# Two chained norms of a residual from sums over the chunks; add, scaling and split chunk by chunk; four chunks of the next map side by side

## The chip, the cores and the metric

The kernel runs on one core of a Trainium2 chip. The metric is the device time of a whole launch in microseconds. Most of the work is on TensorE (matmul); VectorE (DVE in the views) and ScalarE (ACT) prepare its operands and empty its PSUM tiles, SyncE issues the weight loads and GpSimd a few others.

## The reference, cut to what matters

Two diffusion-transformer layers are followed by a third, different block. The residual stream x has 512 latent tokens of 1024 features and, in layer 0, 256 context tokens beside them (768 columns in layer 0, 512 in layer 1). Each layer has two residual additions, and each is followed at once by the norm in front of the next linear map:

```python
xl_new = xl + ml[2] * rmsnorm(y_l, g_post_mix[i])
h2 = modulate(rmsnorm(xl_new, g_pre_mlp[i]), ml[3], ml[4])
xl_new = xl_new + ml[5] * rmsnorm(sqrelu_mlp(h2, w_mlp_in[i], w_mlp_out[i]), g_post_mlp[i])
...
hl = modulate(rmsnorm(xl, g_pre_mix[i]), ml[0], ml[1])   # next layer
zl = hl @ w_in[i]
```

`rmsnorm(u, g)` is `u * rsqrt(mean(u*u) + 1e-6) * g`, the mean over the 1024 features, and `modulate(h, shift, scale)` is `h * (1 + scale) + shift`. All is fp32.

## The kernel before, in words

**Layout.** Features lie on partitions: x is the SBUF tile `X` of 8 chunks of 128 features, each with up to 768 token columns; a branch's output is `Y` of the same form. A sum over features is thus a sum over the 8 chunks and, inside one, over partitions, which a matmul with a tile of ones does.

**Linear maps.** Both operands of a map are split in a high and a low part (`HH`, `HL` for activations, `AHm`, `ALm` inside the MLP, `WH`, `WL` for weights), and three matmuls (lines 555 to 557) stand for one fp32 product. Weights come in slabs of 128x2048; for each slab ScalarE writes `WH` (line 437) and VectorE `WL` (line 448). There are two buffers of each, so a slab can be split only when the last output chunk of the slab two before it is done. A map (`Linear`) makes its output chunks one after the other; with `pair` the first two are made side by side, input chunk by input chunk, so that the map can begin before all eight input chunks are ready. The PSUM ring `psum` has four tiles, one for each chunk under way.

**A residual.** `y` is evicted, squared on ScalarE, the squares are summed over chunks on VectorE (line 616), one matmul with ones sums over partitions (line 624), ScalarE makes `Ln` and then `Exp(-0.5 ...)` of it (lines 651, 658; each with a table load). `vector_add_normed` adds the normed y to X (lines 722, 715); ScalarE squares the new X (line 602), TensorE sums chunk by chunk (line 635), again `Ln` and `Exp`, and `vector_norm_split` scales (line 695) and makes `HL` (line 686), ScalarE `HH` (line 671). Only then the next map starts.

**Order.** Every engine runs an order written out by hand (the functions `tensor_*`, `scalar_*`, `vector_*`), and waits on semaphores; a wait holds all that stands behind it on the engine. The modulation products ("mods", line 477) of the next layer are woven into the weight plan, one behind each slab.

**Names of the stretches.** A is the residual after the mixer of layer 0 (next map: the first `up` map of the MLP), B that after the MLP of layer 0 (next: `w_in` of layer 1), C and D the same two of layer 1 (next: first `up` map, then `win2` of the third block). The MLP is done in 8 groups g; each has an `up` map (4 chunks, 2 slabs) and a `down` map (8 chunks, 2 slabs) that adds to Y. Between them the `up` chunks go through `Relu` on ScalarE (line 1339, which frees the PSUM tile), a square on VectorE (1391), `AHm` on ScalarE (1343) and `ALm` on VectorE (1395), with two buffers `TA`.

Of the kernel before, what the change touches and what calls it, by code (L numbers as in the profile page):

```python
# [529 lines left out]

def tensor_linear(k, pe, L, ring=None):
    ring = ring or k.psum
    for s, g in L.groups():
        if s is not None:
            n = k.slab_of[L.name, s]
            wh, wl = split_views(k, n, L.K)
            mods = list(k.mods[L.name, s])  # L540
# [26 lines left out]
def scalar_linear(k, act, L):  # L567
    for s, g in L.groups():
        if s is not None:
            n = k.slab_of[L.name, s]  # L570
            mods = list(k.mods[L.name, s])
            scalar_split(k, act, n)
            scalar_split(k, act, n + 1)
# [8 lines left out]
def vector_linear(k, dve, L):  # L582
    for s, g in L.groups():
        if s is not None:
            n = k.slab_of[L.name, s]
            mods = list(k.mods[L.name, s])
            vector_split(k, dve, n)
            vector_split(k, dve, n + 1)
# [118 lines left out]
def vector_add_normed(k, dve, name, segs, scale):  # L707

    a, b = span(segs)
    r = k.RS.of(name)  # L710

    def add(c):
        dve.wait_ge("norm_t", (name, c, segs[-1][0]))
        t = k.TD.of((name, c))
        dve.e.tensor_tensor(k.X[:, c, a:b], k.X[:, c, a:b], t[:, a:b], ALU.add).then_inc(*dve.done("x_new", (name, c)))

    for c in range(8):
        t = k.TD.take(dve, (name, c), ("x_new", (name, c)))
        dve.wait_ge("rstd", name)
# [66 lines left out]
def tensor_start(k, pe):  # L786
# [4 lines left out]
    for c in range(8):  # L791
        tensor_stat(k, pe, ("x", 0), c, 8, [LAT, CTX])
# [2223 lines left out]
```

## Time and profile before

| | us |
|---|---|
| median of 3 runs | 4177.93 (4172.32 to 4181.32) |
| the profiled execution, its time | 4172.92 |
| the profiled execution, its span | 4171.6 |
| TensorE busy | 3933.1 (94%) |
| VectorE busy | 2139.4 (51%) |
| ScalarE busy | 1514.4 (36%) |

The span runs from the first to the last instruction; 1.3 us of the launch lie outside it. TensorE is busy almost everywhere, and the stretches A to D are among the places where it is not: between the last matmul of one map and the first of the next one it has only sums to make.

### The profile page before, as it was taken

The page shows a single profiled execution, that of the slowest core. Times are in us where ns is not written, and L with a number is a line of the kernel's source. Part 1 is how long each engine was busy: PE and PEld are TensorE (multiplying, and loading weights), DVE is VectorE, ACT ScalarE, POOL GpSimd, SP SyncE. Part 2 cuts the span into 40 slices and gives each one's busy share as a digit, 9 for nine tenths or more (in the row PEclk, how much of TensorE's full clock was granted, in tenths as well). Part 3 has the DMA queues.
Part 4 walks back from the last instruction along what each step waited for, and adds up shares of the span by engine and source line. Part 5 has one row for each costly group of instructions (what it writes and reads, how often), then busy time and mean ns, then how long its engine had stood idle before and what let it go on. Part 6 is the DMA issues. An engine that isn't in the chain of part 4 may idle for free.

```text
span 4171.6 us, 47663 instructions
## 1 busy us (share of the span) xinstructions
PE 3933.1 (94%) x19722; PEld 3110.9 (75%) x19722; DVE 2139.4 (51%) x3752; ACT 1514.4 (36%) x1872; POOL 494.1 (12%) x748
## 2 busy tenths in 40 slices
PE   6998889999899889999899989999997999999999
PEld 4755768888775568876777878878886788888887
DVE  2275343333447344444554355778873666654444
ACT  3245442212244643234554433344443322222222
POOL 0000000000000000000001000357655111100000
PEclk8999999999999999999999999999999999999999
DMA  5400123332120022222214233345455666543332
GB/s 192 156 26 1 61 81 111 121 112 91 51 76 8 21 71 91 99 83 95 77 41 138 74 116 111 132 162 163 162 174 185 184 185 193 182 146 112 114 126 82
DMA packets 109832, 459.76 MB, mean 110 GB/s; under 512 B 9216, under 2 KB 43120, under 8 KB 68912
## 3 DMA queue, kind: packets, MB, share of 16 engines
q1 hardware_dynamic: 82048, 354.96, 24.5%
q0 software_dynamic: 27568, 101.74, 8.2%
q8 instruction: 156, 2.56, 0.2%
q14 instruction: 60, 0.49, 0.0%
HBM read 389.04 MB, written 67.63 MB: 109 GB/s over the span
## 4 chain that ended last, share of the span: by engine, by line
PE 81%; DVE 8%; ACT 4%; DMA 3%; POOL 2%; issue 1%; SPq 0%; DVEq 0%; ACTq 0%; POOLq 0%
PE ps L557 22%; PE ps L555 22%; PE ps L556 22%; PE ps L2351 2%; DVE ACC L1221 1%; PE ps L1020 1%; POOL Y L2487 1%; PE ps L635 1%; PE ps L477 1%; DVE MX L1194 1%; PE ps L1898 1%; PE ps L1099 1%; DMA stage<-in_w_mod 1%; DVE TD L722 1%; DMA gdram<-GST 1%
## 5 line engine op out<-in xcount | busy, mean ns | idle before, releaser
L555 PE MATMUL ps<-HH,WH 128*128 128x512 f32 x2760 | 1059.1, 384 | 45.8 <-DVE HL L686 36.5
L556 PE MATMUL ps<-HL,WH 128*128 128x512 f32 x2760 | 1048.9, 380 | 0.0
L557 PE MATMUL ps<-HH,WL 128*128 128x512 f32 x2760 | 1048.6, 380 | 0.0
L448 DVE TENSOR_TENSOR WL<-stage,WH 128x2048 fp32r<-128x2048 f32 x248 | 567.4, 2288 | 485.5 <-ACT WH L437 485.5
L437 ACT ACTIVATE WH<-stage 128x2048 fp32r<-128x2048 f32 x248 | 472.8, 1906 | 571.3 <-PE ps L557 528.9
L555 PEld LDWEIGHTS ps<-HH,WH 128*128 128x128 f32 x2760 | 523.7, 190 | 159.0 <-issue 43.6
L557 PEld LDWEIGHTS ps<-HH,WL 128*128 128x128 f32 x2760 | 524.7, 190 | 105.5
L556 PEld LDWEIGHTS ps<-HL,WH 128*128 128x128 f32 x2760 | 523.5, 190 | 103.3 <-issue 1.2
L555 PE MATMUL ps<-AHp,WH 128*128 128x512 f32 x1024 | 407.0, 397 | 7.3 <-ACT Y L2669 7.3
L556 PE MATMUL ps<-ALp,WH 128*128 128x512 f32 x1024 | 406.6, 397 | 0.0
L557 PE MATMUL ps<-AHp,WL 128*128 128x512 f32 x1024 | 406.4, 397 | 0.0
L557 PE MATMUL ps<-AHm,WL 128*128 128x512 f32 (+1 forms) x768 | 275.9, 359 | 0.0
L556 PE MATMUL ps<-ALm,WH 128*128 128x512 f32 (+1 forms) x768 | 275.5, 359 | 0.0
L555 PE MATMUL ps<-AHm,WH 128*128 128x512 f32 (+1 forms) x768 | 274.6, 358 | 0.0
L2686 DVE TENSOR_TENSOR Y<-Y,ps 128x512 f32<-128x512 f32 x248 | 169.0, 685 | 179.5 <-PE ps L557 179.5
L555 PEld LDWEIGHTS ps<-AHp,WH 128*128 128x128 f32 x1024 | 193.3, 189 | 55.0 <-ACT Y L2669 7.7
L557 PEld LDWEIGHTS ps<-AHp,WL 128*128 128x128 f32 x1024 | 193.2, 189 | 47.2
L556 PEld LDWEIGHTS ps<-ALp,WH 128*128 128x128 f32 x1024 | 193.3, 189 | 47.0
L2487 POOL TENSOR_SCALAR OH<-IO,TA 128x128 f32<-128x128 f32 x256 | 169.9, 678 | 276.5 <-ACT TD L2372 238.7
L1402 DVE TENSOR_TENSOR Y<-Y,ps 128x768 f32<-128x768 f32 (+1 forms) x112 | 91.1, 819 | 187.2 <-PE ps L557 186.5
L2381 ACT ACTIVATE GST<-ps 128x1024 f32<-128x1024 f32 x64 | 129.5, 2050 | 134.3 <-DMA gdram<-GST 90.8
L1391 DVE TENSOR_TENSOR TA<-TA 128x768 f32<-128x768 f32 (+1 forms) x64 | 52.8, 825 | 230.1 <-ACT TA L1339 229.3
(369 smaller groups left out, 4934.1 us busy)
## 6 DMA issues: line engine op xcount, KB each, us to landing
stage<-in_w SPq DMA_DIRECT2D x64, 1024.0 KB, 4.9
stage<-in_u SPq DMA_DIRECT2D x64, 1024.0 KB, 4.9
stage<-in_v SPq DMA_DIRECT2D x64, 1024.0 KB, 4.9
stage<-in_w_mod SPq DMA_DIRECT2D x48, 1024.0 KB, 4.9
GR<-gdram POOLq DMA_DIRECT2D x32, 1024.0 KB, 7.9
adram<-GR SPq DMA_DIRECT2D x22, 1024.0 KB, 4.0
AR<-adram POOLq DMA_DIRECT2D x88, 256.0 KB, 3.4
gdram<-GST SPq DMA_DIRECT2D x16, 1024.0 KB, 5.8
```

Of the source, the lines that this page charges most:

```text
L437: act.e.activation(k.WH[o % 2][:, 0:w], k.stage[n % 2][:, 0:w], ACT.Copy).then_inc(*act.done("slab_hi", n))
L448: dve.e.tensor_tensor(k.WL[o % 2][:, 0:w], k.stage[n % 2][:, 0:w], k.WH[o % 2][:, 0:w].bitcast(F32), ALU.subtract).then_inc(*dve.done("sla ...
L477: mm = pe.e.matmul(p[q:q + 32, 0:256], k.csil[:, 2 * kk:2 * kk + 32], w[:, kk, :], start=(kk < 4), stop=(kk >= 4), tile_position=(0, q))
L555: pe.e.matmul(o, wh[:, kk, cs], L.hh[:, kk, z], start=first, stop=False)
L556: pe.e.matmul(o, wh[:, kk, cs], L.hl[:, kk, z], start=False, stop=False)
L557: mm = pe.e.matmul(o, wl[:, kk, cs], L.hh[:, kk, z], start=False, stop=last)
L1391: dve.e.tensor_tensor(t[:, a:b], t[:, a:b], t[:, a:b], ALU.mult).then_inc(*dve.done("relu_sq", (l, g, c)))
L1402: dve.e.tensor_tensor(k.Y[:, c, a:b], k.Y[:, c, a:b], k.psum.of((D.name, c))[:, a:b], ALU.add).then_inc(*dve.done("down", (l, g, c)))
L2351: mm = pe.e.matmul(p[:, 128 * t:128 * t + 128], oh[:, 1, t, :], oh[:, 0, t, :], start=True, stop=True)
L2381: act.e.activation(k.GST.of(key)[:, :, o:o + 8].rearrange("p n t -> p t n"), k.psw.of(("g", tt, b))[:, :].rearrange("p (t n) -> p t n", t= ...
L2487: op = pool.e.tensor_scalar(oh[:, 1, t, :], k.IO[:, :], k.E2[:, tok:tok + 1], None, ALU.is_equal)
L2686: dve.e.tensor_tensor(k.Y[:, c, 0:512], k.Y[:, c, 0:512], k.psn.of((L.name, c))[:, 0:512], ALU.add).then_inc(*dve.done("pd", (g, c)))
```

## The change

**Norms.** While the chunks of y come, three sums over features grow with them: y squared, (g y) squared and x g y, where g is the scale of the post-norm. With them the mean of the new x squared is known before x itself: it is r*r*sum((gy)^2) + 2*r*sum(xgy) + sum(x^2), with r the reciprocal root of y's mean. The sum of x^2 is kept from residual to residual. The last chunks of the three sums are added by `tensor_moments` (small matmuls that fold 768 columns to 192 on four quarters of the partitions, or 512 to 128), the roots are made on the folded form (`Sqrt` and VectorE's reciprocal), and `tensor_rows` spreads them again.

**By chunk.** `vector_add_norm_split` then takes each chunk through the post-norm, the add, the next norm's scaling and the split, in place of two passes over all chunks.

**Side by side.** `pair` becomes `side`: the first four chunks of the first `up` and `down` map of a layer, of `w_in` of layer 1 and of `win2` are made together. Two slabs must be split before an eight-input map of this kind starts, so `scalar_roots` and `vector_roots` hold the split of the second. The mods of group 0 move to later groups, and the norm in front of the first layer also keeps its sum (eight small ScalarE copies).

```diff
+    "sums": ("moments", "rows_mm"),
...
-    def __init__(self, name, nslab, K, ncol, segs, hh, hl, ready, ends, pair=False, order=None):
+    def __init__(self, name, nslab, K, ncol, segs, hh, hl, ready, ends, side=1, order=None):
...
-            g = [c, c + 1] if c == 0 and self.pair else [c]
-            yield (c // self.per if c % self.per == 0 else None), g
+            g = list(range(c, c + (self.side if c == 0 else 1)))
+            yield [d // self.per for d in g if d % self.per == 0], g
...
-            woven(("up", l, g), 2, lambda s: io["w1"][l, 2 * g + s], rest, lambda s: 1)
-            woven(("down", l, g), 2, lambda s: io["w2"][l, 2 * g + s], rest, lambda s: 1)
+            woven(("up", l, g), 2, lambda s: io["w1"][l, 2 * g + s], rest, lambda s: min(g, 1))
+            woven(("down", l, g), 2, lambda s: io["w2"][l, 2 * g + s], rest, lambda s: min(g, 1))
...
+        for s in begun:
+            scalar_split(k, act, k.slab_of[L.name, s])
+        if begun:
+            scalar_split(k, act, k.slab_of[L.name, begun[-1]] + 1)
...
+def vector_sums(k, dve, y, c, a, b):
...
+    for kind, ring in (("xy", k.TD), ("yy", k.TA), ("gy", k.RS)):
+        t, before = ring.of((kind, y, c)), ring.of((kind, y, c - 1))
+        i = dve.e.tensor_tensor(t[:, a:b], t[:, a:b], before[:, a:b], ALU.add)
+    i.then_inc(*dve.done("sq_sum", (y, c)))
...
+def tensor_moments(k, pe, y, d, l, segs):
...
+    p = k.psum.take(pe, ("moments", y), ("summed", y))
+    pe.wait_ge("scale_sq", (l, d))
+    for c in (6, 7):
+        if c == 6:
+            pe.wait_ge("sq_sum", (y, 6))
+        for m, o in enumerate(MOMENTS):
+            if c == 7:
+                pe.wait_ge(*(("xy", (y, 7)) if m == 2 else ("square", ("yy", y, 7))))
...
+                for q in range(4):
+                    mm = pe.e.matmul(p[32 * q:32 * q + 32, z:z + n], w, src[:, s0 + n * q:s0 + n * q + n],
...
+def scalar_roots(k, act, names, segs, slab, ss):
...
+    act.e.activation(t[:, 0:n], p[:, 0:n], ACT.Sqrt, bias=k.epsc[:, 0:1], scale=1.0 / 1024).then_inc(*act.done("root1", y))
+    scalar_split(k, act, slab)
+    act.wait_ge("summed", y)
+    act.e.activation(t[:, 576:576 + n], ss[:, 0:n], ACT.Sqrt, bias=k.epsc[:, 0:1],
...
+def vector_roots(k, dve, names, segs, slab, xx, ss):
...
+    dve.e.reciprocal(r, t[:, 0:n]).then_inc(*dve.done("inverse1", y))
...
+    dve.e.reciprocal(t[:, 0:n], t[:, 576:576 + n]).then_inc(*dve.done("inverse2", y))
+    vector_split(k, dve, slab)
...
+            dve.e.scalar_tensor_tensor(t[:, z], k.Y[:, c, z], gain(c, s0), ry[:, z], ALU.mult, ALU.mult).then_inc(
+                *dve.done("norm_t", (y, c, s0)))
+        dve.wait_ge("norm_t", (y, c, segs[-1][0]))
+        dve.e.tensor_tensor(k.X[:, c, a:b], k.X[:, c, a:b], t[:, a:b], ALU.add).then_inc(*dve.done("x_new", (y, c)))
         if c > 0:
-            add(c - 1)
-    add(7)
+            low(c - 1)
+        u = k.TD.take(dve, (x, c), ("norm_lo", (x, c)))
...
-                  lambda c: [("relu", (l, g, c))], g == 0)
+                  lambda c: [("relu", (l, g, c))], 4 if g == 0 else 1)
...
-                  lambda c: [("down0" if g == 0 else "down", (l, g, c))], True)
+                  lambda c: [("down0" if g == 0 else "down", (l, g, c))], 4 if g == 0 else 2)
```

What this does to the order, at three places. In the rows below a name is out<-in with the tile's buffer number, the numbers behind are partitions x elements, and a line stands for one instruction (lines of the changed kernel have other numbers: 451 is its `WL` split, 742 its x g y, 757 its sums, 857, 860, 868 and 848 its post-norm, add, scaling and `HL`).

**VectorE in stretch A.** Before, from the last chunk's sum of squares to the first adds:

```order
L616 TENSOR_TENSOR TA_58<-TA_58,TA_57 128x768 [waits s_normed,s_rms_rows]
L527 SCALAR_TENSOR_TENSOR AB<-MODs_70,cols_68 128x8 x4
L527 SCALAR_TENSOR_TENSOR AB<-MODs_70,cols_68 128x8 [waits s_scaled]
L527 SCALAR_TENSOR_TENSOR AB<-MODs_70,cols_68 128x8
L722 SCALAR_TENSOR_TENSOR TD_61<-Y,AB,RS_63 128x512 [waits s_rms_rows,s_scaled]
L722 SCALAR_TENSOR_TENSOR TD_61<-Y,AB,RS_63 128x256
L722 SCALAR_TENSOR_TENSOR TD_60<-Y,AB,RS_63 128x512
L722 SCALAR_TENSOR_TENSOR TD_60<-Y,AB,RS_63 128x256
L715 TENSOR_TENSOR X<-X,TD_61 128x768 [waits s_normed]
```

Of the change, in the same place:

```order
L821 RECIPROCAL TA_57<-TA_57 128x192 [waits s_rms_rows,s_scaled]
L823 TENSOR_TENSOR TA_57<-TA_57,ps 128x192 [waits s_normed]
L825 SCALAR_TENSOR_TENSOR TA_57<-ps,TA_57 128x192 [waits s_scaled]
L827 TENSOR_TENSOR TA_57<-TA_57 128x192 [waits s_scaled]
L829 TENSOR_TENSOR ACC<-TA_57,ACC 128x192 [waits s_scaled]
L831 RECIPROCAL TA_57<-TA_57 128x192 [waits s_rms_rows]
L451 TENSOR_TENSOR WL_55<-stage_51,WH_53 128x2048 [waits s_chunk,s_slab_hi]
L857 SCALAR_TENSOR_TENSOR TD_61<-Y,AB,RS_63 128x512 [waits s_rms_rows,s_sums]
L857 SCALAR_TENSOR_TENSOR TD_61<-Y,AB,RS_63 128x256
L860 TENSOR_TENSOR X<-X,TD_61 128x768 [waits s_normed]
L868 SCALAR_TENSOR_TENSOR TD_60<-X,AB,RS_62 128x512 [waits s_normed,s_rms_rows,s_sums]
L868 SCALAR_TENSOR_TENSOR TD_60<-X,AB,RS_62 128x256
```

The chain of the roots, two reciprocals among it, and the split of the second slab (`WL`) now stand ahead of the first post-norm, and each chunk goes on to its scaling at once.

**VectorE in the last `down` map of layer 0.** Before, one chunk's addition to Y is followed by one sum of squares (L616):

```order
L616 TENSOR_TENSOR TA_58<-TA_58,TA_57 128x768 [waits s_rms_rows]
L1402 TENSOR_TENSOR Y<-Y,ps 128x768 [waits s_mix_rows,s_chunk]
L616 TENSOR_TENSOR TA_57<-TA_57,TA_58 128x768 [waits s_normed,s_rms_rows]
L448 TENSOR_TENSOR WL_56<-stage_52,WH_54 128x2048 [waits s_slab_hi]
L1402 TENSOR_TENSOR Y<-Y,ps 128x768 [waits s_mix_rows,s_chunk]
L616 TENSOR_TENSOR TA_58<-TA_58,TA_57 128x768 [waits s_normed,s_rms_rows]
L1402 TENSOR_TENSOR Y<-Y,ps 128x768 [waits s_mix_rows,s_chunk]
```

Of the change, with the split and the chunk behind it:

```order
L742 SCALAR_TENSOR_TENSOR TD_60<-X,AB,Y 128x256
L451 TENSOR_TENSOR WL_56<-stage_52,WH_54 128x2048 [waits s_slab_hi]
L1575 TENSOR_TENSOR Y<-Y,ps 128x768 [waits s_chunk]
L757 TENSOR_TENSOR TD_60<-TD_60,TD_61 128x768 [waits s_rms_rows,s_normed]
L757 TENSOR_TENSOR TA_57<-TA_57,TA_58 128x768
L757 TENSOR_TENSOR RS_62<-RS_62,RS_63 128x768
L742 SCALAR_TENSOR_TENSOR TD_61<-X,AB,Y 128x512 [waits s_normed,s_mix_rows]
L742 SCALAR_TENSOR_TENSOR TD_61<-X,AB,Y 128x256
```

Each chunk now carries three sums and the product x g y.

**ScalarE from the last split of an activation in A to the first `down` map.** Before:

```order
L671 ACTIVATE HH<-TD_60,MODs_70 128x512 [waits s_normed]
L671 ACTIVATE HH<-TD_60,MODs_70 128x256 [waits s_normed]
L437 ACTIVATE WH_53<-stage_52 128x2048 [waits s_slab1]
L501 ACTIVATE mrow_72<-ps 128x256 [waits s_mod_products]
L1339 ACTIVATE TA_57<-ps 128x768 [waits s_chunk]
L1343 ACTIVATE AHm<-TA_57 128x768 [waits s_mix_rows]
L1339 ACTIVATE TA_58<-ps 128x768 [waits s_chunk]
```

Of the change:

```order
L681 ACTIVATE HH<-TD_60,MODs_71 128x512 [waits s_normed]
L681 ACTIVATE HH<-TD_60,MODs_71 128x256 [waits s_normed]
L440 ACTIVATE WH_54<-stage_52 128x2048 [waits s_chunk,s_slab1]
L1506 ACTIVATE TA_58<-ps 128x768
L1510 ACTIVATE AHm<-TA_58 128x768 [waits s_mix_rows]
L1506 ACTIVATE TA_57<-ps 128x768
L1510 ACTIVATE AHm<-TA_57 128x768 [waits s_mix_rows]
L1506 ACTIVATE TA_58<-ps 128x768 [waits s_chunk]
L1510 ACTIVATE AHm<-TA_58 128x768 [waits s_mix_rows]
```

The split of the `down` map's first slab, which waits for a chunk of the `up` map, stands ahead of all four `Relu`; before, ScalarE's `Relu` for chunk 0 waited for chunk 0 alone.

## Rows read from the trace of the kernel before

**Rows 1.** The page, costliest groups: line, engine, operation, tiles, count | busy us, mean ns | idle
```profile
L555 PE MATMUL ps<-HH,WH 128*128 128x512 f32 x2760 | 1059.1, 384 | 45.8 <-DVE HL L686 36.5
...
L448 DVE TENSOR_TENSOR WL<-stage,WH 128x2048 fp32r<-128x2048 f32 x248 | 567.4, 2288 | 485.5 <-ACT WH L437 485.5
...
L437 ACT ACTIVATE WH<-stage 128x2048 fp32r<-128x2048 f32 x248 | 472.8, 1906 | 571.3 <-PE ps L557 528.9
```

**Rows 2.** Timeline, TensorE, stretch A: start us, us, instruction, [idle before, releaser]
```profile
547.93 0.77 PE L555 MATMUL ps<-HH,WH 128*128 128x512 f32 x1 [6.61 <-DVE HL L686]
...
558.68 1.07 PE L477 MATMUL ps<-stage,csil 128*32 128x256 f32 x16
...
586.59 0.39 PE L555 MATMUL ps<-AHm,WH 128*128 128x512 f32 x1
```

**Rows 3.** Timeline, ScalarE, stretch A
```profile
513.23 0.81 ACT L1324 ACTIVATE Y<-ps 128x768 f32<-128x768 f32 x1 [6.78 <-PE ps L557]
...
567.39 0.81 ACT L1339 ACTIVATE TA<-ps 128x768 f32<-128x768 f32 x1 [4.38 <-PE ps L557]
...
569.98 0.79 ACT L1339 ACTIVATE TA<-ps 128x768 f32<-128x768 f32 x1
```

**Rows 4.** Timeline, VectorE, stretch A
```profile
524.28 0.95 DVE L715 TENSOR_TENSOR X<-X,TD 128x768 f32<-128x768 f32 x1
525.27 1.15 DVE L722 SCALAR_TENSOR_TENSOR TD<-Y,AB,RS 128x512 f32<-128x512 f32 x2
...
548.89 1.14 DVE L686 SCALAR_TENSOR_TENSOR HL<-TD,MODs,HH 128x512 fp32r<-128x512 f32 x2
```

**Rows 5.** Timeline, TensorE, stretches B, C and D
```profile
1162.04 0.77 PE L555 MATMUL ps<-HH,WH 128*128 128x512 f32 x1 [6.96 <-DVE HL L686]
...
1192.50 0.40 PE L555 MATMUL ps<-HH,WH 128*128 128x512 f32 x1
...
1483.19 1.10 PE L624 MATMUL ps<-TA,ones 128*128 128x512 f32 x2 [2.16 <-DVE TA L616]
...
1505.39 0.77 PE L555 MATMUL ps<-HH,WH 128*128 128x512 f32 x1 [5.27 <-DVE HL L686]
...
1529.53 0.40 PE L555 MATMUL ps<-AHm,WH 128*128 128x512 f32 x1
...
1868.61 1.10 PE L624 MATMUL ps<-TA,ones 128*128 128x512 f32 x2 [2.92 <-DVE TA L616]
...
1890.54 0.64 PE L555 MATMUL ps<-HH,WH 128*128 128x512 f32 x1 [5.08 <-DVE HL L686]
...
1915.55 0.40 PE L555 MATMUL ps<-HH,WH 128*128 128x512 f32 x1
```

**Rows 6.** Timeline, VectorE, last down map of layer 0
```profile
1113.65 2.29 DVE L448 TENSOR_TENSOR WL<-stage,WH 128x2048 fp32r<-128x2048 f32 x1 [2.78 <-ACT WH L437]
...
1126.00 0.95 DVE L1402 TENSOR_TENSOR Y<-Y,ps 128x768 f32<-128x768 f32 x1 [2.41 <-PE ps L557]
```

**Rows 7.** Groups by form, VectorE reciprocals: busy us, mean ns
```profile
L1199 DVE RECIPROCAL MX<-MX 128x4 f32<-128x4 f32 x8 | 1.4, 170 | 1.1 <-ACT G L1135 1.1
...
L1979 DVE RECIPROCAL BIG<-BIG 128x8 f32<-128x8 f32 x4 | 0.8, 203 | 0.1
```

**Rows 8.** Timeline, TensorE, runs of small fp32 matmuls
```profile
1428.53 1.04 PE L1059 MATMUL ps<-ident,MX 128*64 128x128 f32 x16
...
1995.60 1.64 PE L1884 MATMUL ps<-KCM,QN 128*128 128x32 f32 x14
```

**Rows 9.** Timeline, VectorE, layer 1, first up map
```profile
1518.15 0.69 DVE L1391 TENSOR_TENSOR TA<-TA 128x512 f32<-128x512 f32 x1
...
1520.15 0.69 DVE L1391 TENSOR_TENSOR TA<-TA 128x512 f32<-128x512 f32 x1
```

**Rows 10.** Stretch after the first matmul of A: busy times, granted clock (PEclk)
```profile
547.93:551.33 3.40, 3.40 (x10) 2.83 (x11) 3.37 (x7) 1.60 (x3) 0.00 (x0) 0.50 0.00 0
```

**Rows 11.** Timeline, ScalarE, first normalization of the program
```profile
64.22 2.13 ACT L671 ACTIVATE HH<-TD,MODs 128x512 fp32r<-128x512 f32 x4 [0.97 <-DVE TD L695]
```

More of the change, by code:

```diff
@@ L567, in scalar_linear @@
 def scalar_linear(k, act, L):
[L568 to L573, printed above, removed]
+    for begun, g in L.groups():
+        mods = [m for s in begun for m in k.mods[L.name, s]] + (mods if not begun else [])
+        for s in begun:
+            scalar_split(k, act, k.slab_of[L.name, s])
+        if begun:
+            scalar_split(k, act, k.slab_of[L.name, begun[-1]] + 1)
         while mods and len(g) == 2 and L.K == 8:
@@ L582, in vector_linear @@
 def vector_linear(k, dve, L):
[L583 to L588, printed above, removed]
+    for begun, g in L.groups():
+        mods = [m for s in begun for m in k.mods[L.name, s]] + (mods if not begun else [])
+        for s in begun:
+            vector_split(k, dve, k.slab_of[L.name, s])
+        if begun:
+            vector_split(k, dve, k.slab_of[L.name, begun[-1]] + 1)
         while mods and len(g) == 2 and L.K == 8:
@@ L704, in norm_end, with scalar_y_squares @@
     return "norm_t", (name, n - 1, segs[-1][0])
-def vector_add_normed(k, dve, name, segs, scale):
+def scalar_y_squares(k, act, y, d, c, segs):
     a, b = span(segs)
[L710 to L719, printed above, removed]
+    act.wait_ge("scale", (y[1], d, 1))
+    over = ("sq_sum", (y, c + 1)) if c < 6 else ("moments", (y, c))
+    t = k.TA.take(act, ("yy", y, c), over)
+    act.e.activation(t[:, a:b], k.Y[:, c, a:b], ACT.Square).then_inc(*act.done("square", ("yy", y, c)))
+    if c < 7:
+        t = k.RS.take(act, ("gy", y, c), over)
+        for (s0, sn) in segs:
+            z, v = slice(s0, s0 + sn), which(s0)
+            i = act.e.activation(t[:, z], k.Y[:, c, z], ACT.Square, scale=k.AB[:, d, c, v:v + 1])
+        i.then_inc(*act.done("square", ("gy", y, c)))
@@ new lines, in vector_xy @@
+def vector_xy(k, dve, y, d, c, segs):
+    dve.wait_ge("scale", (y[1], d, 1))
+    t = k.TD.take(dve, ("xy", y, c), ("sq_sum", (y, c + 1)) if c < 6 else ("moments", (y, c)))
+    for (s0, sn) in segs:
+        z, v = slice(s0, s0 + sn), which(s0)
+        if c < 7:
+            i = dve.e.scalar_tensor_tensor(t[:, z], k.X[:, c, z], k.AB[:, d, c, v:v + 1], k.Y[:, c, z], ALU.mult, ALU.mult)
+        else:
+            i = dve.e.tensor_tensor(t[:, z], k.X[:, c, z], k.Y[:, c, z], ALU.mult)
+    i.then_inc(*dve.done("xy", (y, c)))
@@ new lines, in tensor_rows @@
+def tensor_rows(k, pe, names, i, segs):
+    p, t = k.psum.take(pe, ("rows", names[i]), ("rstd", names[i])), k.TA.of(("roots", names[0]))
+    pe.wait_ge(("inverse1", "inverse2")[i], names[0])
+    for (s0, sn) in segs:
+        n, o = sn // 4, 192 * (1 - i) + s0 // 4
+        for q in range(4):
+            mm = pe.e.matmul(p[:, s0 + n * q:s0 + n * q + n], k.ident[:, 32 * q:32 * q + 1].broadcast_to([128, 128]),
+                             t[:, o:o + n], start=True, stop=True)
+    mm.then_inc(*pe.done("rows_mm", names[i]))
@@ L791, in tensor_start @@
     for c in range(8):
[L792 removed]
+        tensor_stat(k, pe, ("x", 0), c, 8, [LAT, CTX], keep=True)
+    k.psum.give(("stat", ("x", 0)), ("xx", 0))
 def gain_of(k, d):
@@ L1302, in tensor_mix @@
             pass
-    tensor_stat_sum(k, pe, ("ymlp", l), segs)
-    for c in range(8):
-        tensor_stat(k, pe, ("x", l + 1), c, 8, segs)
+    tensor_moments(k, pe, ("ymlp", l), 3, l, segs)
+    for i in range(2):
+        tensor_rows(k, pe, residual(l, 1), i, segs)
     pe.mark(f"layer{l}")
```

225 lines of the change are left out of this document (159 added, 66 removed).

## The prediction

> **What bounds the kernel now.** I read the page's groups first, then the timeline of TensorE where it was idle, then ScalarE and VectorE around one such place. TensorE is 94% busy; the linear maps' first matmul (L555) was idle 45.8 us in all, 36.5 of it for `HL` [rows 1]. In stretch A the last chunk of y reaches ScalarE at 513.23 and the next map's first matmul starts at 547.93, held by `HL` [rows 2, 3]: 34.7 us. The same is B from 1126.0 to 1162.04 [rows 5, 6], C from 1481.0 (1483.19 less 2.16 of idle) to 1505.39, and D from 1865.7 (1868.61 less 2.92) to 1890.54 [rows 5]. These four gaps, some 120 us, are what the change works on. But the worth of an edit is read where TensorE is again as far as before. In A that is the first `down` matmul, 586.59 [rows 2], in B the fifth chunk of `w_in`, 1192.50, in C the first `down` matmul, 1529.53, in D the fifth chunk of `win2`, 1915.55 [rows 5].
>
> **Unit prices.** One input chunk of one output chunk costs TensorE 1.06 us in layer 0: A takes 38.66 us for 32 of them [rows 2], less two mods of 1.3 (1.07 and its transposes [rows 2]), less 2.2 for the slow clock. After the idle of A the granted clock was 0.50, that is 1.2 GHz, for 3.4 us [rows 10], and climbed in the next, which I put at 2.2 us for each cold start. For 512 columns it is 0.70. A weight slab's split is 1.91 on ScalarE and 2.29 on VectorE [rows 1].
>
> **The chain to the first post-norm, A.** The chain of squares, log and exp twice goes (four table loads with it), and so does one pass over X. In its place stands:
> - `tensor_moments`, 48 small matmuls, 96 records. A run of 16 small ones took 1.04 us [rows 8], 65 ns each, some 62 without the last one's drain. 96 records are 6.0 us, from 513.2 to 519.2; the last square and product of y are ready before their turn.
> - `Sqrt` of 192 columns, 0.45 with its wait: 519.65.
> - The reciprocal. Its rows are 170 ns for 4 columns and 203 ns for 8 [rows 7], 8.3 ns for each further column, where an add of 768 takes 0.95 us [rows 4], 1.2 ns. 192 columns come to 1.73 us: 521.4. At the add's rate it would be 0.35; I take the reciprocal's own rows.
> - Four small operations of 0.39 each, the second `Sqrt` 0.45 and the second reciprocal 1.75: 525.15. ScalarE's slab split lies beside them.
> - VectorE's split of the second slab, 2.2 in front of the post-norm: 527.3. Rows for x (16 records, some 2 us, and a copy) are hidden behind it and the first add.
>
> **The loop.** A chunk now costs VectorE post-norm 1.15, add 0.95, `HL` 1.14, scaling 1.15 [rows 4], 4.4 in all, and the first `HL` comes after one and a half rounds, 6.6. So TensorE starts at 533.9, 14.0 sooner. Four chunks side by side want 4.24 per input chunk, less than VectorE's 4.4, so VectorE sets the pace and part of the cold start stays: the four are done at 569.8. The scales moved behind the loop cost nothing: VectorE would wait there for the split.
>
> **The handover, the step that decides.** Before, chunks came one by one and `Relu`, square, `AHm`, `ALm` of one lay beside the next. Now all four end within 3.2 us. ScalarE's next instruction is the `down` slab's split; it waits for the second chunk (567.7), ends at 569.6, and VectorE's part at 571.9. Behind it the four activations go in turn: the cycle is 2.7 (567.39 to 569.98, [rows 3], with the ring's wait). The fourth `Relu` ends at 580.1. The first `down` map is four wide as well and takes all four PSUM tiles at once, so TensorE waits for that `Relu`: 10.3 us idle, and it starts cold, 2.2. Compare 582.3 with 586.59 less the two mods that only move to later groups, 584.0: A gains **1.7**, of a head start of 14.0.
>
> **B.** In the last `down` map of layer 0 VectorE has per chunk the addition 0.87, three sums of 0.87 and x g y 1.1, 4.7 with waits, and TensorE needs 4.24. At the fifth chunk ScalarE's split stands behind the squares, which wait for the sums: where VectorE idled 2.78 before [rows 6] and caught up, it idles 2.9 and does not. From the start at 1092.1 (1126.0 less 8x4.24) I get sums(3) 21.2, x g y 22.2, the split from 25.1 to 27.3, then four rounds, to 45.2: sums(6) end at 1137.3, 11 us behind TensorE. Moments (6.0) end at 1143.3, the chain of A (8.1) gives 1151.4, the first matmul comes at 1158.0, 4.0 sooner. `w_in` wants 3.5 per input chunk, VectorE gives one in 4.4: the four end at 1190.6. The third slab's split waits for the second chunk and two memsets: 2.8 more, 1193.4 against 1192.50: **loses 0.9**.
>
> **C and D.** With 128 folded columns: moments 3.0, reciprocal 1.2, small ones 0.32, loop 2.95. C: 1484.1, first post-norm 1490.9, first matmul 1495.4 (10 sooner), four done at 1519.6. Handover: split until T+2.8, three cycles of 2.0 [rows 9], T+8.8, cold 2.2: 1530.6 against 1529.53, **loses 1.1**. D: VectorE's backlog in the last `down` map by the sum of B, 3.2 per chunk against 2.8 and the split, puts sums(6) at 1875.2, the first matmul at 1889.5 (1.0 sooner), four done at 1913.8, the third slab 2.8 later: 1916.6 against 1915.55, **loses 1.0**.
>
> **The start.** Eight small copies (some 2 us) stand on ScalarE before the first `HH`, which would begin 0.97 after VectorE's first row [rows 11]: **loses 0.9**. GpSimd's loads for the third block go out earlier, under stretch D, where the slabs are already there: nothing; without that cover a slab would be late by a few us. The mods in later groups cost what they did.
>
> **Sum.** -1.7 +0.9 +1.1 +1.0 +0.9 = **+2.2 us** on 4172.92 of the profiled execution, 4175.1. That execution stands 5.0 under the median of the runs, 4177.93, so the median comes to 4180. No change: some 29 us of head start are given back at the four ends.
>
> **Where a rule of the skill bears.** The moments' pitch in the rows is 62 ns [rows 8]. The Trainium skill, "TensorE: Matmul & The Clock Gate", section "Wait — 56ns, not 53.3ns?", gives a floor of about 25 ns from start to start, and 62 ns only where the sequencer's microcode decodes; the rows of this kernel agree with the latter. By the lower one the sum would be about 10 us better. The long reciprocal agrees with "VectorE: DVE Perf Modes", which says that it iterates with a repeat count of 8.
>
> **Rivals.** (1) *Moments at the array's pace* (chance 0.12). The mod's 16 records of 256 columns on four column tiles took 1.07 us, 67 ns each [rows 2]; if the pitch follows the columns, 128 and 64 of them need 17 to 33, on average some 27. For it: that row is the only one on four tiles. Against it: the 16 of 128 columns on two tiles were no faster [rows 8]. 35 ns less on 96, 96, 48 and 48 records: -10. With the sum: -8, 4170, at the edge of faster. (2) *The handover is hidden* (0.15). If the `down` map could start when chunk 0's `ALm` is there, or cycles were shorter, A and C would keep 7 more each, and if VectorE kept up in the last `down` maps, B and D 6 and 4 more: -24, with the sum -22, 4156. Against it: the order on ScalarE and the four tiles. (3) *Moments held by their weight loads* (0.15), the other side. A row of matmuls with few columns took 1.64 us for 14 records [rows 8], 105 ns pitch net of the drain; at that the four stretches lose 4.1, 4.1, 2.1, 2.1: +12, with the sum +14, 4192. It decides above about 90 ns a record. (4) *The reciprocal at one column a cycle* (0.08): -2.8, -2.8, -1.8, -1.8 = -9, 4171. (5) *Backlogs longer* (0.08): a wait of 0.5 more in each round of B and D, +5 in all, +7: 4185. My forecast has 0.42.
>
> **How the numbers follow.** About 0.2% (8.4 us) is what a measurement of this kernel tells from no change. The forecast with its errors (some 6 us) and rivals 4 and 5 lie mostly within; rival 1 falls on both sides of the edge, 2 is faster, 3 slower. Faster is rival 2, half of rival 1 and 0.08 from the tails of the forecast and rival 4, 0.29; slower is rival 3 and 0.08 from the tails of the forecast and rival 5, 0.23; the rest, 0.48, is no change. The likeliest case has 4173 to 4187; the range for 8 in 10 takes in rivals 1 and 4 and most of 2 and 3: 4161 to 4192.
>
> **What would show it.** TensorE's first `up` matmul in A some 14 us after, not 35 less a little: gap of about 21 us, and then a second gap of about 10 in front of the first `down` matmul, ended by ScalarE's `Relu`. In the last `down` map of layer 0, VectorE without idle time and sums(6) about 11 us after TensorE's last matmul. A reciprocal of 192 columns near 1.7 us. Wrong would be: no second gap, a reciprocal of 0.35, records of the moments at 35 or over 90 ns, or VectorE level with TensorE in B.

## The result and the profile after

The changed kernel takes **4155.61 us** (median of 5 runs, 4153.41 to 4158.48) against 4177.93 for the kernel before; the ratio is 0.9947 with a 95% interval of 0.9933 to 0.9962. It is faster by some 22 us, where no change was forecast, and lies below the range. All times are of undisturbed executions; one slow one (5812.29 us at a granted clock of 0.62, the fourth of the last kernel) is left out of that kernel's times.

The page of the changed kernel, for [rows 1] (L566 is the old L555):

```profile
span 4157.2 us, 48351 instructions
...
L566 PE MATMUL ps<-HH,WH 128*128 128x512 f32 x2760 | 1060.0, 384 | 49.6 <-DVE HL L848 20.7
...
L566 PE MATMUL ps<-AHm,WH 128*128 128x512 f32 (+1 forms) x768 | 276.0, 359 | 19.6 <-DVE ALm L1568 19.6
```

The idle time put down to `HL` fell from 36.5 to 20.7 us, but that of the whole line did not, and the `down` maps now have 19.6 us of their own: the second gap. TensorE's timeline at the places of [rows 2] and [rows 5] (start, us, instruction, idle before and its releaser; L777 are the moments, L790 the rows):

```profile
516.57 0.54 PE L777 MATMUL ps<-TA,ones 128*32 128x128 f32 x16
516.92 0.51 PE L777 MATMUL ps<-RS,ones 128*32 128x128 f32 x16
517.25 0.51 PE L777 MATMUL ps<-TD,ones 128*32 128x128 f32 x16
...
534.18 0.77 PE L566 MATMUL ps<-HH,WH 128*128 128x512 f32 x1 [5.34 <-DVE HL L848]
...
580.76 0.77 PE L566 MATMUL ps<-AHm,WH 128*128 128x512 f32 x1 [10.52 <-DVE ALm L1568]
...
1132.16 0.86 PE L777 MATMUL ps<-TA,ones 128*32 128x128 f32 x16 [11.42 <-DVE RS L757]
...
1150.80 0.77 PE L566 MATMUL ps<-HH,WH 128*128 128x512 f32 x1 [5.34 <-DVE HL L848]
...
1186.76 0.47 PE L566 MATMUL ps<-HH,WH 128*128 128x512 f32 x1 [3.11 <-ACT ZQ L1006]
...
1524.24 0.76 PE L566 MATMUL ps<-AHm,WH 128*128 128x512 f32 x1 [9.07 <-DVE ALm L1568]
...
1864.30 0.65 PE L777 MATMUL ps<-TA,ones 128*32 128x128 f32 x8 [11.16 <-DVE RS L757]
```

A run of 16 moments starts 0.33 to 0.35 us after the last: 22 ns a record on average, not 62. (In the trace the four records on the four quarters of the partitions start 6 to 7 ns apart, and 36 to 113 ns pass before the next four.) In B the runs start 0.62 to 0.65 us apart, 40 ns a record, at a granted clock of 0.50, the lower level. TensorE in the moments of B and in the first of A (the window, busy us and records, granted clock, DMA share, GB/s):

```profile
1132.16:1135.30 3.14, 3.14 (x80) 0.50 0.02 5
516.57:517.70 1.13, 1.13 (x49) 1.00 0.00 0
```

The handover in A is idle for 10.52 us (forecast 10.3), and the sums in B end some 11 us behind TensorE (forecast 11). ScalarE in the handover of A shows why it waits, against [rows 3]:

```profile
516.67 0.81 ACT L1495 ACTIVATE Y<-ps 128x768 f32<-128x768 f32 x1 [5.40 <-PE ps L568]
...
568.25 1.92 ACT L440 ACTIVATE WH<-stage 128x2048 fp32r<-128x2048 f32 x1 [6.50 <-PE ps L568]
570.07 0.79 ACT L1506 ACTIVATE TA<-ps 128x768 f32<-128x768 f32 x1
...
574.14 0.79 ACT L1506 ACTIVATE TA<-ps 128x768 f32<-128x768 f32 x1
...
576.88 0.79 ACT L1506 ACTIVATE TA<-ps 128x768 f32<-128x768 f32 x1
...
579.61 0.79 ACT L1506 ACTIVATE TA<-ps 128x768 f32<-128x768 f32 x1
```

The slab's split stands ahead of the four `Relu`, the fourth of them starts at 579.61, and the first `down` matmul follows 1.15 us later. The view puts that matmul's wait down to `ALm`, but VectorE's first `ALm` had ended at 575.22, 5.5 us before:

```profile
574.26 0.96 DVE L1568 TENSOR_TENSOR ALm<-TA,AHm 128x768 fp32r<-128x768 f32 x1 [0.91 <-ACT AHm L1510]
```

The fourth `Relu`, which frees the fourth PSUM tile, ended 0.36 us before. VectorE has the long reciprocal at 1.35 us (forecast 1.73):

```profile
520.26 1.35 DVE L821 RECIPROCAL TA<-TA 128x192 f32<-128x192 f32 x1 [1.56 <-ACT TA L802]
```

**A second cold start.** The forecast has a wait of 2.8 us at the third slab of `w_in` and `win2`, and nothing behind it. The wait is there (3.11 us in B), and behind it the granted clock falls once more. TensorE in B and in D:

```profile
1186.76:1188.50 1.74, 1.74 (x6) 0.74 0.29 61
1188.50:1190.20 1.70, 1.70 (x5) 0.50 0.99 410
...
1908.00:1910.00 2.00, 2.00 (x7) 0.50 0.97 410
```

Seven matmuls in B and eight in D take 427 ns from start to start in place of 227 and 233, about 1.5 us each time. The kernel before has no such wait there and runs at 1.00 (1192.50 to 1198.50 and 1915.55 to 1919.50).

**Where the 22 us are.** So the mechanism of the four stretches is nearly the forecast one, and the time is not. I numbered the 13,800 main matmuls of both kernels in order of time and compared their starts. The mean time from one start to the next is called the pitch below. Far from the four stretches, in code that the diff doesn't touch, the changed kernel gains all the time. TensorE alone in two windows without any idle time (us, busy us and matmuls, granted clock, DMA share, GB/s), before and then after:

```profile
1620.00:1820.00 200.00, 200.00 (x858) 1.00 0.27 95
3500.00:4000.00 500.00, 500.00 (x2136) 1.00 0.44 143
```

```profile
1620.00:1820.00 200.00, 200.00 (x884) 1.00 0.28 100
3500.00:4000.00 500.00, 500.00 (x2145) 1.00 0.44 142
```

In the first window (MLP of layer 1, all matmuls of 512 columns) 858 became 884 at the same granted clock of 1.00: from start to start 233.3 ns before and 226.7 after. In the third block it is 234.3 and 233.3, in the MLP of layer 0 (512 and 256 columns by turns) 176.7 and 175.1 on average. Times their numbers, some 4,130 matmuls in layer 0 by 1.6 ns, 2,110 in layer 1 by 6.6 and 7,560 behind by 1.0, that is 6.6 + 13.9 + 7.6 = 28 us: more than the whole gain.

What differs for these matmuls? The change allocates one small buffer, `last_gain`, 32 bytes of each partition. All buffers behind it stand 32 bytes further on, among them the ones that the main matmuls stream: divided by 128 bytes, the addresses of `HH`, `HL`, `AHm`, `ALm` (layers) go from a remainder of 96 to 0, those of `HH2`, `HL2`, `AHp`, `ALp` (third block) from 32 to 64. **Theory P** is that this place sets the pitch. Rivals: **C**, the pitch is a state of the run and the chains gave the gain; **W**, the changed order of waits in the map loop gave it.

### The profile page after: what moved, and what is told of

Same layout as the page of the kernel before. It is cut to its first block, busy times and chain, and to the rows that moved or that the text cites. A ratio compares the mean times of both kernels' runs of the same rounds, so it can differ in the third digit from the quotient of the medians.

```text
span 4157.2 us, 48351 instructions
## 1 busy us (share of the span) xinstructions
PE 3895.5 (94%) x19998; PEld 3108.8 (75%) x19998; DVE 2220.1 (53%) x3875; ACT 1493.4 (36%) x1876; POOL 493.3 (12%) x748
## 4 chain that ended last, share of the span: by engine, by line
PE 78%; DVE 10%; ACT 5%; DMA 3%; issue 2%; POOL 1%; SPq 0%; DVEq 0%; ACTq 0%; POOLq 0%
PE ps L566 21%; PE ps L567 21%; PE ps L568 21%; PE ps L2533 1%; PE ps L1176 1%; DMA gdram<-GST 1%; DVE ACC L1377 1%; DVE WL L451 1%; PE ps L480 1%; PE ps L645 1%; POOL Y L2669 1%; DVE MX L1350 1%; PE ps L1255 1%; ACT WH L440 1%; PE ps L2080 1%
## 5 line engine op out<-in xcount | busy, mean ns | idle before, releaser
L566 PE MATMUL ps<-HH,WH 128*128 128x512 f32 x2760 | 1060.0, 384 | 49.6 <-DVE HL L848 20.7
L566 PEld LDWEIGHTS ps<-HH,WH 128*128 128x128 f32 x2760 | 525.8, 191 | 160.2 <-issue 47.2
L566 PE MATMUL ps<-AHp,WH 128*128 128x512 f32 x1024 | 404.4, 395 | 7.9 <-ACT Y L2851 7.9
L566 PE MATMUL ps<-AHm,WH 128*128 128x512 f32 (+1 forms) x768 | 276.0, 359 | 19.6 <-DVE ALm L1568 19.6
L566 PEld LDWEIGHTS ps<-AHp,WH 128*128 128x128 f32 x1024 | 192.0, 188 | 55.8 <-ACT Y L2851 8.3
L566 PEld LDWEIGHTS ps<-AHm,WH 128*128 128x128 f32 x768 | 146.3, 191 | 42.2 <-ACT TA L1506 20.2
```

Of the source, the lines that this page charges most:

```text
L566: pe.e.matmul(o, wh[:, kk, cs], L.hh[:, kk, z], start=first, stop=False)
```

## Experiments: the place of the streamed tensors

**32 bytes more, and nothing else** (kernel before).

```
     k.cols2 = new("cols2", [128, 32])
+    k.pad = new("pad", [128, 8])
```

> The kernel before, with one unused buffer of 32 bytes per partition allocated where the changed kernel has its last_gain; the order of every instruction is that of before. Every buffer allocated behind it (HH, HL, AHm, ALm among them) stands 32 bytes further on, where it is in the changed kernel. Theory P (the place of the streamed buffers sets the pitch of the main matmuls: 233.4 ns a matmul of 512 columns before, 226.7 in the changed kernel, in the same code of layer 1): pitch 226.7 in layer 1 and 233.3 in the third block, and a time some 20 us under before, about 4157. Theory C (the shorter chains of the four stretches gave the 22 us, and the pitch is a state of the run): time of before, 4178 within 8 us, pitch 233.4. Theory W (pitch depends on the changed order of waits in the map loop): also the time of before.

Measured: 4150.78 us, ratio 0.9938 (0.9924 to 0.9952): 26.5 us under the runs of before beside it (4177.32). Pitches 175.1, 226.7 and 233.3 ns, as in the changed kernel. No instruction was moved, so C and W fall, and the padded kernel is even 5 to 7 us faster than the changed one.

**Another 32 bytes in the changed kernel.**

```
     k.last_gain = new("last_gain", [128, 8])
+    k.pad = new("pad", [128, 8])
```

> The changed kernel with another unused 32 bytes behind last_gain, so that the buffers behind it stand at the same remainder of 64 bytes as before the change. Theory P: the pitch in layer 1 goes from 226.7 back to 233.4 ns, in the third block from 233.3 to 234.3, and the time from 4155.6 up to some 4176 to 4181: the chains alone are worth about nothing, as the prediction's sum of +2.2 us had it. Theory C: 4155.6 as the changed kernel.

Measured: 4171.06 us, ratio 0.9983 (0.9974 to 0.9991). Layer 1 is back at 233.3 ns, as expected; but layer 0 stays at 174.9 and the third block at 233.3. A remainder of 64 was the wrong key: 64 bytes from before is another place, not the old one. The pitches alone should give 4,130 by 1.8 and 7,560 by 1.0 ns, 15 us, and 6.3 came: the rest of the change costs some 9 here.

**Both kernels once more.**

> The kernel before, unchanged, for the run to run scatter and for the pitch. Theory P: 233.4 ns in layer 1 and 234.3 in the third block again, ratio 1.000 within 0.1%. If the pitch were a state of the run, a second profile would have a chance to show 226.7.

> The changed kernel, unchanged. Theory P: 226.7 ns in layer 1 and 233.3 in the third block again, time 4155.6 within 3 us. If the pitch were a state of the run it may show 233.4.

Measured: 4177.85 us (ratio 1.0005, 0.9996 to 1.0014) and 4157.40 us (0.9953, 0.9940 to 0.9967), with their old pitches to 0.1 ns, so these two pitches are no state of one execution.

**HH and HL alone** (kernel before): which buffer is it?

```
-    h = Room(nc, z.at)
+    h = Room(nc, z.at + 32)
```

> The kernel before with HH and HL alone 32 bytes further on, from byte 175200 to 175232 of each partition, a multiple of 128; AHm and ALm and all else stay at a remainder of 96. Theory P (the place of the tensor that a matmul streams sets its pitch): in the MLP of layer 1 the up maps, which stream HH and HL, at 226.7 ns, the down maps, which stream AHm and ALm, still at 233.4; about half of the gain in the layers, some 8 to 10 us of 4177. Rival A (the place of some other buffer behind the pad, which the engines write beside the matmuls): both kinds of map stay at 233.4, time 4177. Rival W (whichever): both at 226.7.

Measured: 4161.20 us, ratio 0.9958 (0.9945 to 0.9972). That is 12 to 23 us, more than the 8 to 10 expected; the pitches alone give 13 (2,592 matmuls on `HH` and `HL` in layer 0 by 1.7 ns, 1,344 in layer 1 by 6.4). TensorE's timeline, the first matmul of an `up` map, of the `down` map behind it and of the next `up` map in layer 1:

```profile
1587.74 0.39 PE L555 MATMUL ps<-HH,WH 128*128 128x512 f32 x1
...
1609.52 0.40 PE L555 MATMUL ps<-AHm,WH 128*128 128x512 f32 x1
...
1631.92 0.39 PE L555 MATMUL ps<-HH,WH 128*128 128x512 f32 x1
```

Each map has 96 matmuls: 21.78 us for `up`, 226.9 ns each, and 22.40 us for `down`, 233.4. Only the maps whose stream was moved are faster, in layer 0 too (175.0 ns on `HH` and `HL`, 176.6 on `AHm` and `ALm`). P holds tensor by tensor, in one trace.

**32 bytes lower, and both groups at 128** (kernel before). The 32 bytes of `epsc` go to the end of the memory; the second kernel also leaves a gap of 64 ahead of the layers' buffers (`AHm` and `ALm` move with them).

```
-    k.epsc = new("epsc", [128, 1])
+    k.epsc = nc.alloc_sbuf_tensor_at("epsc", [128, 1], F32, offset=229312)
...
-    z = Room(nc, r.at)
+    z = Room(nc, r.at + 64)
```

> The kernel before with its 32 byte constant epsc moved to the end of the memory, so that every buffer behind it stands 32 bytes lower: HH2, HL2, AHp and ALp of the third block at a multiple of 128 (before: remainder 32), HH, HL, AHm and ALm of the layers at a remainder of 64 (before: 96). Theory P128 (226.7 ns needs a multiple of 128): layers 233.3, third block 226.7 instead of 234.3, some 7500 matmuls by 7 ns, 50 us: about 4125. Theory P64 (a multiple of 64 is enough in the layers, and the third block has a bound of its own): layers 226.7, third block 233.3, about 4155, as with 32 bytes more.

> The kernel before with epsc at the end and 64 bytes of gap ahead of the buffers of the layers: HH2, HL2, AHp, ALp, HH, HL, AHm and ALm all at multiples of 128 bytes; the order of every instruction is that of before. Theory P128: 226.7 ns in the layers and in the third block: the 26 us of the 32 byte kernel and some 50 more, about 4100. Theory P64: no more than the 32 byte kernel, 4151.

Measured: 4150.22 us (0.9932, 0.9919 to 0.9946) and 4146.90 us (0.9922, 0.9908 to 0.9935). Theory P128 was half right: the third block gets faster with a multiple of 128 (232.4 ns), but not to 226.7. All places that ran, with the remainders by 128 bytes of the tensors of the layers and of the third block, and the pitches in ns (the third block's is that of its last part, from about 3240 us on):

| kernel | layers | third block | layer 0 | layer 1 | third block | us |
|---|---|---|---|---|---|---|
| before | 96 | 32 | 176.7 | 233.3 | 234.3 | 4177.9 |
| before, 32 more | 0 | 64 | 175.1 | 226.7 | 233.3 | 4150.8 |
| before, HH and HL 32 more | 0 and 96 | 32 | 175.0 and 176.6 | 226.9 and 233.4 | 234.3 | 4161.2 |
| before, 32 less | 64 | 0 | 174.0 | 233.3 | 232.4 | 4150.2 |
| before, both at 128 | 0 | 0 | 175.0 | 226.7 | 232.4 | 4146.9 |
| changed | 0 | 64 | 175.1 | 226.7 | 233.3 | 4155.6 |
| changed, 32 more | 32 | 96 | 174.9 | 233.3 | 233.3 | 4171.1 |
| changed, both at 128 (below) | 0 | 0 | 175.0 | 226.7 | 233.3 | 4147.9 |
| the same, two wide (below) | 0 | 0 | 175.0 | 226.7 | 232.4 | 4141.8 |

The last column comes from different sets of runs. The kernel before had medians of 4177.3 to 4180.4 in them, so 3 us between two rows tell nothing by themselves. And one row does not fit: with all tensors at 128, the changed kernel has 233.3 ns in the last part of the third block, while the kernel below it, whose buffers stand at the same addresses and which differs in one map of each layer, has 232.4. TensorE in one window there, the first kernel and then the second:

```profile
3500.00:4000.00 500.00, 500.00 (x2144) 1.00 0.42 141
```

```profile
3500.00:4000.00 500.00, 500.00 (x2153) 1.00 0.42 141
```

So in the third block, at a remainder of 0, the place is not all that sets the pitch. It changes inside one execution too: the kernel before with both at 128 has 233.3 from 2543 to 2632 us and mostly 232.4 elsewhere. What else sets it is open. In the layers no run contradicts the place.

## Experiments: the chains of the four stretches

**The changed kernel at 128** (`last_gain` in a dead part of `fold`; the rest of the edit as above).

```
-    k.last_gain = new("last_gain", [128, 8])
...
+    k.last_gain = k.fold[:, 0:8]
```

> The changed kernel with all streamed tensors at multiples of 128 bytes (epsc at the end, a gap of 64 ahead of the buffers of the layers, last_gain in the dead part of fold). Against the kernel before so placed, 4146.9, it shows the chains alone. By the pair at 32 bytes more (4150.8 without the change, 4157.4 and 4155.6 with it) the chains cost 5 to 7 us: 4152 to 4154. By the pair at the old remainder (4177.3 and 4171.1) they gain 6: 4141.

Measured: 4147.87 us, ratio 0.9923 (0.9909 to 0.9936), against 4146.90 of the kernel before so placed: +1, with the higher of the two pitches in its third block, which is worth some 3.6 us of its profiled execution (3,970 matmuls by 0.9 ns). So the change without its 32 bytes costs 5 to 7 us at one place and about nothing at another; at neither is a gain seen. By stretch, from numbered matmuls ahead of and behind each, the changed kernel less the one before at the same place (three pairs: two runs of the changed one against 32 more, and the pair at 128):

| | forecast | pairs |
|---|---|---|
| start, to the middle of w_o in layer 0 | +0.9 | +2.0, +1.6, +2.4 |
| A, with the moved mods paid back | -1.7 | -3.8, -4.0, -3.9 |
| B | +0.9 | +2.1, +2.2, +2.2 |
| C | +1.1 | +0.7, -0.8, +1.1 |
| D | +1.0 | +3.8, +3.9, +2.1 |
| sum | +2.2 | +4.8, +2.9, +3.9 |

Two executions of the changed kernel differ by 2.0 us between the same matmuls in the mixer of layer 0 and by 3.6 in that of layer 1, so the row of the start tells nothing against the forecast. The scatter in C comes from `w_o` in front of it: counted from the middle of that map, C is -0.7, -0.7 and -0.5. In D the third pair is 1.6 lower because the second cold start is missing: TensorE at 1908 to 1910 us of the changed kernel at 128 has a granted clock of 1.00, where the changed kernel at its own place has 0.50.

**The handover.** The first `down` map two wide again.

```
-                  lambda c: [("down0" if g == 0 else "down", (l, g, c))], 4 if g == 0 else 2)
+                  lambda c: [("down0" if g == 0 else "down", (l, g, c))], 2)
```

> The changed kernel with the first down map of each layer two chunks side by side, as before the change, instead of four; the first up map stays four wide. TensorE then needs two of the four PSUM tiles at first. If the handover (10.5 us idle in A, 9.1 in C, ended by ALm) is held by the fourth Relu, as the prediction had it: the idle times fall by one and a half to two Relu cycles each, 4 to 5 us in A and 3 to 4 in C, and the time by 5 to 9, to some 4149 to 4152. If it is held by the first ALm: no change, or a loss of a few us where two wide runs out of input chunks (each is then asked for in 2.1 us, and arrives every 2.7).

Measured: 4150.41 us, ratio 0.9930 (0.9916 to 0.9943), 5 to 7 under the changed kernel. TensorE in A and C:

```profile
576.05 0.77 PE L566 MATMUL ps<-AHm,WH 128*128 128x512 f32 x1 [5.12 <-DVE ALm L1568]
...
1517.57 0.77 PE L566 MATMUL ps<-AHm,WH 128*128 128x512 f32 x1 [5.11 <-DVE ALm L1568]
```

10.5 and 9.1 us of idle time became 5.1 each: the wait was for PSUM tiles behind the fourth `Relu`. What is left is the first `ALm` behind the slab's split. By numbered matmuls of the profiled executions A is 4.7 us shorter, C 1.2.

**The same at 128.**

> The changed kernel with both edits that helped: streamed tensors at multiples of 128 bytes, and the first down map of each layer two chunks wide. The two are independent, so 4157.4 less 6 for the handover and less 4 for the third block: 4147, level with the kernel before at 128 (4146.9) and 30 under the kernel before.

Measured: 4141.82 us, ratio 0.9913 (0.9900 to 0.9927); 6 under the changed kernel at 128, and 5 under the kernel before there, where 4147 was expected. In the traces A gives 4.9 of it and C 3.0; another 3.7 is the pitch of the third block, which the edit does not touch, and the profiled execution of the changed kernel at 128 was its slowest.

**The backlog: one of three sums on GpSimd** (a new `pool_sums`, called behind `pool_att`; VectorE leaves that sum out for `ymlp`).

```
+        pool.e.tensor_tensor(t[:, a:b], t[:, a:b], before[:, a:b], ALU.add).then_inc(*pool.done("gy_sum", (y, c)))
...
+    for kind, ring in (("xy", k.TD), ("yy", k.TA), ("gy", k.RS))[:2 if y[0] == "ymlp" else 3]:
```

> The changed kernel with one of VectorE's three sums (that of the squares of g y) in the last down map of each layer done on GpSimd instead; all else as it is, buffers at their places. VectorE then has about 3.8 us a chunk there in layer 0 against TensorE's 4.2, where it had 4.7. If VectorE's throughput makes the idle time of some 11 us that TensorE has in B and in D ahead of the moments (ended by the sums): both fall, B to some 6 and D to some 7, and the time by 8 to 10 us, to about 4147. If GpSimd's add is slower than a chunk's 4.2 us (its operations on 128 columns took 0.66 to 0.68 us, at that rate 4 us for 768), its chain of sums is late instead, and the idle times grow.

Measured: 4163.77 us, ratio 0.9962 (0.9948 to 0.9975): 6 to 8 slower than the changed kernel. GpSimd, and then VectorE, in the last `down` map of layer 0:

```profile
1102.17 2.66 POOL L760 TENSOR_TENSOR RS<-RS,RS 128x768 f32<-128x768 f32 x1 [3.72 <-ACT RS L735]
```

```profile
1102.18 0.95 DVE L773 TENSOR_TENSOR TD<-TD,TD 128x768 f32<-128x768 f32 x1
1103.05 2.61 DVE L773 TENSOR_TENSOR TA<-TA,TA 128x768 f32<-128x768 f32 x1
```

The add on GpSimd was not so slow, 1.8 to 2.7 us where I expected 4. But VectorE's second add beside it took 2.61 us in place of 0.95, and so (2.56 to 2.61) in four of the six chunks: what was taken off VectorE came back as longer adds. Each of these four ended 0.8 us after GpSimd's add. TensorE's idle time ahead of the moments grew from 11.4 to 13.0 in B, and from 11.2 to 12.5 in D. That is under 3 us of the loss; the rest stands in the third block, where the code is the same and no cause was found.

**The backlog: no sums** (the two wide kernel at 128 with the moments of all chunks on TensorE; `XYs` and `YYs` lie where `HH` and `HL` are, which are free there, and GpSimd's load of `W1`, whose place overlaps theirs, waits for the moments).

```
+def tensor_moments_apart(k, pe, y, d, segs):
...
+    for c in range(8):
+        for m, o in enumerate(MOMENTS):
+            pe.wait_ge(*(("xy", (y, c)) if m == 2 else ("square", ("yy", y, c))))
+            src = (k.XYs if m == 2 else k.YYs)[:, c, :]
...
-                    vector_sums(k, dve, ("ymlp", l), c - 1, a, b)
...
-                vector_xy(k, dve, ("ymlp", l), 3, c, segs)
+                dve.e.tensor_tensor(k.XYs[:, c, a:b], k.X[:, c, a:b], k.Y[:, c, a:b], ALU.mult).then_inc(
+                    *dve.done("xy", (("ymlp", l), c)))
```

> The kernel of e12 without VectorE's sums in the last down map of each layer: squares and products of all eight chunks of y are kept apart where HH and HL are free, and TensorE takes the moments from all of them (192 small matmuls in layer 0, 96 in layer 1, instead of 48 and 24). VectorE has then 1.8 us a chunk there and ScalarE 0.8. If VectorE's backlog makes the 11.4 us that TensorE is idle ahead of the moments in B and the 11.2 in D: that idle time is gone but for a fraction of a microsecond, the moments of the first seven chunks take 168 records by 22 ns, 3.7 us, in B and 1.8 in D, the last ones end 4.4 us behind the map in B and 2.4 in D (now 12.5 and 11.9), and the first matmuls of w_in and win2 come some 8 and 9 us sooner; 4141.8 less 17 is 4125. If the head start is lost at the third slab again, as in the changed kernel (3.1 us each), this is in both numbers already. If the wait has another cause: 4142.

Measured: a ratio of 0.9877 (0.9857 to 0.9897) from three runs, 4120.32, 4120.43 and 4129.53. The profiled span is 4119.0 us against 4135.2 of the two wide kernel: 16.2 less, 17 were expected. The edit takes more than the sums off the engines: the square of g y on ScalarE goes, and x y needs no factor g on VectorE, since the moments' weights carry it. TensorE has no wait ahead of the moments any more. Its timeline at the last matmul of the `down` map in B and the first moments, at the first matmul of `w_in` and at its third slab, and the latter two for `win2`:

```profile
1114.29 0.28 PE L570 MATMUL ps<-AHm,WL 128*128 128x256 f32 x1
1114.50 0.54 PE L797 MATMUL ps<-YYs,ones 128*32 128x128 f32 x16
...
1137.22 0.76 PE L568 MATMUL ps<-HH,WH 128*128 128x512 f32 x1 [5.28 <-DVE HL L868]
...
1173.21 0.77 PE L568 MATMUL ps<-HH,WH 128*128 128x512 f32 x1 [3.11 <-ACT ZQ L1026]
...
1851.35 0.76 PE L568 MATMUL ps<-HH,WH 128*128 128x512 f32 x1 [4.54 <-DVE HL L868]
...
1878.88 0.47 PE L568 MATMUL ps<-HH,WH 128*128 128x512 f32 x1 [3.10 <-DVE WL L453]
```

By numbered matmuls B is 8.7 us shorter than in the two wide kernel and D 9.4. This kernel beats both the one before and the changed one: some 50 us under the one before, of which about 30 are the place of the tensors. The 3.1 us at the third slab remain in B and D.

## Why the prediction was wrong, point by point

- **The step that failed** is one that the sum does not have: that a main matmul takes as long after the change as before ("one input chunk of one output chunk costs TensorE 1.06 us", taken over for the changed kernel). It is 0.4 to 2.8% shorter, by 32 bytes that the diff adds to the memory map. Priced alone that is -26.5 us; the forecast had 0. I read the line with `last_gain` as a copy of 8 columns, not as a move of all that stands behind it. The trace of before holds only a hint of such a price (233.3 ns in layer 1 and 234.3 in the third block for the same instruction at the same clock); a list of the streamed tensors' addresses would have shown that it moves.
- **The sum of the chains was right, in part by luck**: no gain. Errors of both signs cancel: A came out 2.2 us better than forecast and C (counted from the middle of `w_o`) 1.7, B 1.3 and D 1 to 3 worse. The sum has +3 to +5 us by stretch against +2.2, and +1 to +7 between whole kernels of one placement. What is between stretches and whole is a few us of scatter in the third block, of which the pitch that changes at a remainder of 0 is one part (some 3.6 us in one pair); the rest I can't assign to anything.
- **Moments**: 22 ns a record on average, not 62; rival 1 was right in the pitch at full clock, not in the 10 us: in B the clock was at 0.50 and a record took 40 ns. The mod's run with 67 ns [rows 2] streams 256 columns, and I took the runs on one or two tiles [rows 8] as nearer. The Trainium skill, "TensorE: Matmul & The Clock Gate", section "Wait — 56ns, not 53.3ns?", has about 25 ns as a floor from start to start. The trace lies below it, with 22 on average and 6 to 7 inside a group of four, and far from that page's 62. The first `up` matmul of A came 17.5 us after the last chunk, not 20.7; of these 3.2 us A kept 2.2, 3.9 instead of 1.7.
- **Reciprocal**: 1.35 us for 192 columns, not 1.73, and far from the add's 0.35. Rival 4 falls.
- **The handover** was as forecast, place, price and cause (10.52 of 10.3 us; half of it gone with two wide). That it is avoidable (close to rival 2's condition) is shown too, and is worth 6 us, not the 14 I gave it in A and C.
- **VectorE's backlog** was as forecast in B (11.4 of 11 us). In D it is 11.2, where I had put sums(6) at 1875.2, some 9.5 behind TensorE. That the sums, with the square and the product beside them, make it was shown by leaving them out.
- **B and D** lost 2.2 and 2.1 to 3.8 us, not 0.9 and 1.0. The term put at nothing is the cold start behind the wait at the third slab, about 1.5 us each; the one trace in which D is without it has the 2.1.
- **Rival 2 named nearly the right time (4156) for a wrong reason**: neither was the handover hidden nor did VectorE keep up.

## What to carry to other kernels

Before costing an edit, list the address of every tensor that TensorE streams, before and after, also where the diff only adds a small buffer; and when a comparison is in, look at the pitch of untouched matmuls first. To measure such a change, run it beside the old kernel padded by the same bytes. Shortening a chain ahead of a map that starts from several side by side chunks gives its gain back at the other end if the map behind needs all PSUM tiles at once, and sums in front of a matmul by ones are better left to TensorE if it would wait for them.

## What the runs showed of the hardware

- In this kernel the start-to-start time of a matmul of 512 fp32 columns at granted clock 1.00 went with the byte address of the streamed tensor: in the layers (rows of 3072 bytes) 226.7 ns at a multiple of 128 and 233.3 at remainders of 32, 64 and 96; in the third block (rows of 2048 bytes) 233.3 at 64 and 96, 234.3 at 32, and at 0 both 232.4 and 233.3 (in its last part 232.4 in four kernels and 233.3 in a fifth). With 256 and 512 columns by turns the order is another: 174.0 at 64, 174.9 at 32, 175.1 at 0, 176.7 at 96. Why the third block does not come to 226.7 is open; whether the length of the rows or the distance of the tensors does it wasn't tried.
- A `tensor_tensor` add of 768 columns on VectorE beside one on GpSimd took 2.56 to 2.61 us in place of 0.95, and GpSimd's 2.62 to 2.66 where it took 1.84 to 1.85 in the other two chunks. This was seen in four of six chunks.
- Small matmuls (128 or 64 fp32 columns on 32 output rows, four quarters in turn) ran at 22 ns a record on average at granted clock 1.00 and at 40 ns at 0.50.
- After an idle time of 3.1 us TensorE ran its next matmuls at 1.00, and then the granted clock fell to 0.50, where matmuls of 512 columns took 427 ns from start to start (B in all traces of the changed kernel and its variants, D in all but one).
